# A bidirectional RWKV recurrence laid out anew: direction by half of the partitions, one Gram product for b and k

## The reference, cut to what matters

```
def step(s, inp):
    r_t, w_t, k_t, v_t, a_t, b_t = inp
    sa = jnp.einsum('bhvk,bhk->bhv', s, a_t)
    s = s * w_t[:, :, None, :] + sa[..., :, None] * b_t[:, :, None, :] + v_t[..., :, None] * k_t[:, :, None, :]
    return s, jnp.einsum('bhvk,bhk->bhv', s, r_t)
```

## Time and profile before

| | us |
|---|---|
| median of three runs | 2892.38 |
| the profiled execution | 2887.43 |
| its span, first to last instruction | 2885.4 |
| parameters and first modulation | 0 to 51 |
| projection, to its barrier | about 51 to 460.0 |
| recurrence, to its barrier | 460.1 to 1050.7 |
| the rest (heads, experts, second block) | 1050.7 to 2885.4 |

### The profile page before, as it was taken

The page is one execution under the profiler, slowest core; times in us unless marked ns, Lnnn a source line. Parts: engine busy times, 40 slices in busy tenths (PEclk is TensorE's granted clock), DMA queues, the critical chain, the costliest instruction groups (busy, mean ns, idle before and its releaser), DMA issues. The chain is left out here.

```text
span 2885.4 us, 56115 instructions
## 1 busy us (share of the span) xinstructions
PE 2368.4 (82%) x23980; PEld 1971.1 (68%) x23980; DVE 1720.8 (60%) x2490; ACT 1204.6 (42%) x2180; POOL 612.4 (21%) x528
## 2 busy tenths in 40 slices
PE   5799995889999979692699999998229999777889
PEld 5677785788888857581477777777217777655767
DVE  1555565666666527427588788888346757354652
ACT  2421212444444322242477777777233232255430
POOL 0300002444344300114010111110333544100000
PEclk9799997999999989796799999999659999899999
DMA  5222221110101044336389999998573343000032
GB/s 196 69 71 64 67 65 61 47 47 33 47 33 47 18 151 156 119 124 247 132 329 348 347 352 336 338 349 310 158 262 99 89 146 102 31 1 1 1 124 110
DMA packets 147234, 406.06 MB, mean 141 GB/s; under 512 B 9878, under 2 KB 38700, under 8 KB 146988
## 3 DMA queue, kind: packets, MB, share of 16 engines
q1 hardware_dynamic: 131500, 350.04, 34.0%
q0 software_dynamic: 10880, 39.85, 5.2%
q10 hardware_dynamic: 4608, 12.58, 1.1%
HBM read 350.01 MB, written 52.43 MB: 139 GB/s over the span
## 5 line engine op out<-in xcount | busy, mean ns | idle before, releaser
L1632 DVE TENSOR_TENSOR exp_w_lo<-exp_w,exp_w_hi 128x4096 fp32r<-128x4096 f32 x93 | 410.3, 4424 | 120.1 <-ACT exp_w_hi L1589 118.0
L1589 ACT ACTIVATE exp_w_hi<-exp_w 128x1024 fp32r<-128x1024 f32 x384 | 373.4, 1048 | 175.6 <-DMA exp_w<-in_exp_w_down_dram 91.0
L1958 PE MATMUL bank<-w_hi,h_lo 128*128 128x512 f32 (+1 forms) x448 | 175.4, 391 | 34.3 <-DMA h_lo<-h_tiles 26.1
L1927 POOL TENSOR_TENSOR w_lo<-heads_a,w_hi 128x512 fp32r<-128x512 f32 (+1 forms) x104 | 138.4, 1357 | 184.8 <-ACT w_hi L1973 184.7
L1555 PE MATMUL bank<-exp_w_hi,xsT_lo 128*128 128x512 f32 x512 | 162.2, 398 | 13.5 <-DVE exp_w_lo L1632 7.6
L1958 PE MATMUL bank<-w_hi,h_hi 128*128 128x512 f32 (+1 forms) x448 | 171.6, 383 | 0.0
L1958 PE MATMUL bank<-w_lo,h_hi 128*128 128x512 f32 (+1 forms) x448 | 171.6, 383 | 0.0
L1555 PE MATMUL bank<-exp_w_lo,xsT_hi 128*128 128x512 f32 x512 | 159.3, 393 | 0.0
L1555 PE MATMUL bank<-exp_w_hi,xsT_hi 128*128 128x512 f32 x512 | 158.8, 391 | 0.0
L787 DVE TENSOR_TENSOR w<-bank,const 128x256 f32<-128x256 f32 x200 | 75.4, 419 | 119.5 <-PE bank L1008 119.5
L1523 POOL DMA_INDIRECT moe_rows<-exp_out,idxT x16 | 25.3, 1579 | 562.2 <-DVE exp_out L1683 562.2
(11 more groups left out here) (341 smaller groups left out, 6210.3 us busy)
## 6 DMA issues: line engine op xcount, KB each, us to landing
exp_w<-in_exp_w_gate_dram SPq DMA_DIRECT2D x32, 2048.0 KB, 8.3
exp_w<-in_exp_w_up_dram SPq DMA_DIRECT2D x32, 2048.0 KB, 27.7
exp_w<-in_exp_w_down_dram SPq DMA_DIRECT2D x32, 2048.0 KB, 13.2
heads_a<-in_w_in_dram SPq DMA_DIRECT2D x96, 256.0 KB, 2.8
chunk<-rkv_scratch SPq DMA_DIRECT2D x40, 512.0 KB, 4.1
ada_w_second<-in_ada_w_dram SPq DMA_DIRECT2D x8, 2048.0 KB
w_in_ring<-in_w_in_dram SPq DMA_DIRECT2D x26, 512.0 KB, 4.0
ada_w_first<-in_ada_w_dram SPq DMA_DIRECT2D x4, 2048.0 KB, 11.2
```

Of the source, the lines that this page charges most:

```text
L1589: last = act.activation(wh[:, n % RH, k, :], w[:, n % RING, k, :], ACT.Copy)
L1632: dve.tensor_tensor(wl[:, n % RH, :, :], w[:, n % RING, :, :], wh[:, n % RH, :, :], ALU.subtract).then_inc(lo_ok, 1)
L1927: pool.tensor_tensor(wl[:, q % SR, 0:width(q)], w[:, q % WR, 0:width(q)], wh[:, q % SR, 0:width(q)], ALU.subtract).then_inc(w_lo, 1)
L1958: mm = pe.matmul(g.ps[m % 4][:, 0:cols], lhs[:, t % HT, k, :], rhs[:, q % SR, 0:cols], start=(k == 0 and p == 0), stop=(k == KT - 1 and p ...
```

## The change

1. **Layout.** The forward direction lies on partitions 0 to 63 and the backward direction on 64 to 127; the 8 heads stand side by side. Elementwise work that differed by direction is now one instruction over both (one scan of 512 instead of two of 256), but what writes only one half of the partitions is done twice, once for each half.
2. **Gram.** `bk` holds b, k, b; one product with 128 stationary columns (b and k) gives the rows of both at once. 32 products of 64*64 with 192 moving columns become 16 of 64*128.
3. **128 rows.** `gram[d]` has b's part on one half of the partitions and k's on the other, `uv[d]` has u over v, `sv[d]` state over v. So `r0` and `carry` need one product of 128 rows where they had two of 64, `outputs` one of 64 and one of 128 rows where it had three of 64. The ScalarE copies `a` and `end` into `gram[d]` for that.
4. **v turned in the projection.** TensorE transposes v there (40 transposes), ScalarE copies it out of PSUM in 12 pieces, GpSimd stores it to `v_turned` with 8 DMAs. The recurrence loads it; the 16 products that turned v in each turn are gone, and the mask over their result with them.
5. **Logits** are 32 products of 64*64 on four corners instead of 16 of 64*128.
6. **Parameters** by direction: 12 small DMAs are added in `phase_params` and `w0` is taken out of the old list.

```
@@ phase_params, sync @@
+            for n, name in enumerate(("w0", "a0", "k_a")):
+                for d in range(2):
+                    for half in range(2):
...
+                        sp.dma_start(prow2[row:row + HP, d * C:(d + 1) * C], ...).then_inc(loaded, 16)
@@ phase_project @@
+    FIRST = order.index(("rw", 8))
+    pieces = {n: range(2 * (n - FIRST - 2), 2 * (n - FIRST - 1)) for n in range(FIRST + 2, NT - 1)}
+    pieces[NT - 1] = range(2 * (NT - FIRST - 3), 3 * HP)
+    BLOCKS_OF = (range(0, 4), range(4, 8), range(8, 10))
@@ gpsimd, after the loop over the kept blocks @@
+            for j in range(HP):
+                store_values(j)          # waits for vcopied 3 * j + 3, two DMAs
+            for r in range(2):
+                pool.wait_ge(vstored[r], 32 * HP // 2)
@@ scalar, at block n @@
+                for q in pieces.get(n, ()):
+                    vj, blocks = q // 3, BLOCKS_OF[q % 3]
+                    act.wait_ge(vturned, q + 1)
+                    if vj >= 2:
+                        act.wait_ge(vstored[vj % 2], 32 * (vj // 2))
+                    act.activation(turned_values(vj)[...], g.ps[6 + q % 2][:, 0:len(blocks) * P], ACT.Copy).then_inc(vcopied, 1)
@@ vector, before the mix of a kept block @@
+                        if 10 <= j:
+                            dve.wait_ge(vturned, 3 * (j - 10) + 3)
@@ tensor, after the products of block n @@
+                for q in pieces.get(n, ()):
+                    j, blocks = q // 3, BLOCKS_OF[q % 3]
+                    pe.wait_ge(mixed, FIRST + 1 + j)
...
+                    for k, b in enumerate(blocks):
+                        mm = pe.transpose(g.ps[6 + q % 2][:, k * P:(k + 1) * P],
+                                          mix[:, kept_no[8 + j] % MR, b * P:(b + 1) * P], g.c("ident"))
@@ phase_wkv, scalar: copies into gram[d] @@
+                for d in range(2):
+                    ins = act.activation(v.gram[d][:, 2 * p:2 * p + 2, 2],
+                                         banks[d][:, 0:6 * C].rearrange("p (h a t) -> p h a t", h=2, a=3)[:, :, 2], ACT.Copy)
...
+                    for d in range(2):
+                        ins = act.activation(v.gram[d][HALVES[d], :, 0], v.are[h // 2 % 2][HALVES[d], :, 0], ACT.Copy)
@@ phase_wkv, tensor @@
-                signal(quads(small(s, "P"), [(b.are[i][:, :, 0], state[d][s % 2]) for d, b in enumerate(bs)],
-                             [(b.gk[:, :, 0], b.vT) for b in bs]), s, pe_done)
+                for n in range(NH):
+                    for d in range(2):
+                        mm = pe.matmul(v.B[0][HALVES[d], n * C:(n + 1) * C], v.gram[d][:, n, 0], v.sv[d][:, n], start=True, stop=True)
+            def solve(s):
+                        mm = pe.matmul(v.B[1][HALVES[d], n * C:(n + 1) * C], v.y[HALVES[d], n], v.r0[HALVES[d], n], start=True, stop=True)
+            def carry(s):
+                        mm = pe.matmul(v.B[2][HALVES[d], n * C:(n + 1) * C], v.gram[d][:, n, 2], v.uv[d][:, n], start=True, stop=True)
+            def outputs(s):
+                for j in range(HP):
+                    for half in range(2):
+                        n = HP * half + j
+                        for d in range(2):
+                            pe.matmul(v.B[d][HALVES[half], j * C:(j + 1) * C], v.sv[d][HALVES[d], n], v.are[s // 2 % 2][HALVES[d], n, 1],
+                                      start=True, stop=False)
+                        for d in range(2):
+                            mm = pe.matmul(v.B[d][HALVES[half], j * C:(j + 1) * C], v.uv[d][:, n], v.gram[d][:, n, 1], start=False, stop=True)
+            def products(s):
+                        mm = pe.matmul(v.B[3][HALVES[d], n * C:(n + 1) * C], v.are[s // 2 % 2][HALVES[d], n, 0], v.bk[HALVES[d], n, 0],
+                                       start=True, stop=True)
+            def gram(s, p):
+                        mm = pe.matmul(banks[d][:, 3 * j * C:3 * (j + 1) * C], v.bk[HALVES[d], n, d:d + 2].rearrange("p a t -> p (a t)"),
+                                       v.are[s // 2 % 2][HALVES[d], n].rearrange("p a t -> p (a t)"), start=True, stop=True)
+            def logits(s):
+                            for k in range(2):
+                                mm = pe.matmul(v.Q[k][HALVES[d], n * C:(n + 1) * C], up[HALVES[k], d, c0:c0 + C], g.lora[HALVES[k], c:c + C],
+                                               start=True, stop=True)
```

More of the change, by code:

```diff
@@ L570, in ny, with heads @@
         return (s - NCC) // 2 + 1 if s >= NCC else 0
[L572 to L579 removed]
+    def heads(ap):
+        return ap.rearrange("p (h t) -> p h t", t=C)
     def inside(s):
@@ L718, in taken, with turned @@
[L718 to L721 removed]
+            def turned(s, l):
+                v = group[s % 2]
+                act.wait_ge(pe_done[s % 2], at("pe", s, f"t{l}"))
+                act.activation(v.t[:, :, :, :].rearrange("p j d t -> p (j d t)"), v.Q[0][:, :], ACT.Copy).then_inc(act_done[s % 2], 1)
@@ L871, in _ @@
                 if inside(h + 1):
-                    masked(h + 1, "turnv", "turn")
-                if inside(h + 3):
-                    logits(h + 3, 0)
-                    logits(h + 3, 1)
+                    gram(h + 1, 0)
+                    gram(h + 1, 1)
                 if inside(h):
                     level(h, 4)
+                if inside(s):
+                    dve.wait_ge(exp_done[s % 2], th(s))
+                    n = mark(dve.scalar_tensor_tensor(v.sw, v.a, 1.0, v.pi, ALU.add, ALU.mult))
+                    for d in range(2):
+                        ins = dve.tensor_copy(end[HALVES[d], :], v.gx[HALVES[d], :, 0 if d else C - 1])
+                    ins.then_inc(ends_ok[s % 2], 1)
@@ L888, in _ @@
         def _(pe):
-            def quads(outs, *terms, hps=range(HP)):
-                ends = [None, None]
-                for h in hps:
-                    for i, term in enumerate(terms):
-                        for flip in range(2):
-                            for j in range(2):
-                                half = HALVES[(j + flip) % 2]
-                                st, mv = term[j]
-                                moving = mv[half] if len(mv.shape) == 2 else mv[half, h]
-                                ends[j] = pe.matmul(outs[j][half, h - hps[0]], st[half, h], moving, start=(i == 0), stop=(i == len(terms) - 1))
-                return ends
@@ L1024, in join @@
-                signal(ends, s, pe_done)
+                pe.wait_ge(act_done[s % 2], at("act", s, f"t{l}"))
+                pe.wait_ge(dve_done[s % 2], at("dve", s, f"w{l}"))
+                for j in range(HP):
+                    for d in range(2):
+                        for par in range(2):
+                            mm = pe.matmul(v.Q[par][HALVES[d], j * C:(j + 1) * C], v.t[HALVES[par], j, d], v.w[HALVES[par], d, j],
+                                           start=True, stop=True)
```

704 lines of the change are left out of this document (351 added, 353 removed).

## The result

The changed kernel takes 2904.6 us (median of 9 runs, 2900.3 to 2911.0), the kernel before 2890.2 us (9 runs, 2885.0 to 2901.3): ratio 1.0045, interval 1.0027 to 1.0062. It is slower by 14 us, 0.5%, at the edge of what the prediction called no change; its sum had +2. The profiled execution took 2901.9 us against 2887.4.

The account below looks back on a forecast made before the run. TensorE was taken as the bound, by a small margin. Recurrence -8, projection +6 and start +4 summed to +2 us: 2889 us in the profiled execution's terms, 2894 us as median; range of 8 in 10, 2854 to 2924 us.

Parts of the forecast that it names:

- Start: Before the projection: 11 more loads, 0.34 us apart, all landing before anything starts: +3.7 us (bounds 2 and 6).
- Projection: Whole stage: transposes ahead of the last product block +2.2 us, later v stores +3.7: +6 (bounds +2 and +12).
- GpSimd must store v: End of projection: v stores follow ScalarE's last copies and land 12.6 us after the last product, against 8.9: +3.7.
- The case given for the upper end: End of projection: ScalarE's third v waits for a slot whose store has not landed; the stage's +12 us bound.
- Prologue: Turns before turn 0, at half clock: logits 1.9 us instead of 3.5, v's turning gone: -4 us in the chain.
- Turns 5 to 16: Recurrence turns with outputs: 22.1 us of TensorE work plus waits give 28.1 us against 27.8; +4 us over twelve turns.
- Turns 1 to 4: Recurrence turns without outputs: level-3 products wait for y2; 24.1 us against 25.9; with turn 0, -8 us.
- The last three turns: End of the recurrence: no change, 0 us.
- Rival 1: Outputs: changes of shape inside are free, 2.8 us instead of 5.0, -35 us in all: 2859 us; chance 0.2.
- Rival 2: Solve and a-by-b product: halves sharing a PSUM bank go in turn, 1.86 us not 0.93: 2916 us; 0.3 with Rival 3.
- Rival 3: Recurrence: ScalarE and VectorE take 1 us a turn longer than walked: 2912 us; chance 0.3 together with Rival 2.
- Rival 4: TensorE: the change doesn't save the products it says; no size and no chance of its own given.

Follow-up runs that it names:

- experiment 4: Changed kernel with ScalarE's and VectorE's lists reordered: 2848.5 us; with outputs also regrouped, products of 64 rows before those of 128: 2811.6 us.
- experiment 5: Changed kernel with small parameter loads issued from two queues and the first two turned v's stored early: 2895.8 us; with reordered lists and regrouped outputs too: 2803.6 us.
- experiment 7: Changed kernel without the turning of v (no transposes, copies or waits for them; stores stay, recurrence reads other values): 2901.5 us, ratio 1.0035.
- experiments 1 and 2: Changed kernel with ScalarE's copy y4 ahead of e2: 2888.7 us; changed kernel with four or two unneeded products ahead of z5: 2924.9 or 2896.5 us.
- experiment 3: Changed kernel with outputs' four 64-row products together, then four of 128 rows, 8 changes of shape instead of 16: 2881.1 us, ratio 0.9981.

## Why the prediction was nearly right, and by what

Its time was 2894 us, its range 2854 to 2924; 2904.6 us lies inside. That the 12% less of TensorE's work in a turn (22.1 us for 25.0 in the forecast) comes back as waits on the lists of ScalarE and VectorE is right, and experiment 4 shows it from the other side: with other lists the same products give 56 us, 13 of them by the clock in turns 5 to 16. The size of the difference is less good: +2 us were summed and 14.7 measured. Of the 13 us between the two, 5.4 are the projection, 4.2 the prologue, 0.9 the turns and 2.5 what lies behind them, which the sum doesn't have and whose cause is open. By its steps:

- **Start, +3.7 us:** measured 3.7.
- **Projection, +6 (bounds 2 and 12):** measured 11.4. The step that failed is "GpSimd must store v", which placed the stores behind the copies alone: GpSimd's list has even the first v's store behind its last mix, at 453.59, so the slot that the third v needs comes free late. The case given for the upper end came true: ScalarE's third v waits 2.8 us for it (experiment 5 gives 3.0 us back). The last raw copy to the barrier is 7.3 us longer, for 3.7 forecast. Of the rest, 1.9 us are transposes between products (forecast 2.2), and 1.9 us come from the last eight blocks, which take 14.0 us each instead of 13.76 without any transpose; experiment 7 keeps this, and its cause is open.
- **Prologue, -4:** measured +0.2. The logits did gain 3.4 us, but they were not all of the chain: TensorE waits 4.4 us longer for the features, and later 3.6 us for the first end copies. That the features come later because they are now one piece for both directions is likely, and no run tests it.
- **Turns 5 to 16, 28.1 us:** measured 27.7, which hides two errors of opposite sign. At full clock they are 26.6. The scan was priced at 2.6 us, as two of 256 and with GpSimd beside them, and takes 1.23, which leaves 0.5 to 0.8 of the 2.2 us of wait ahead of join 2. TensorE's own work is 0.7 us more than the 22.1 priced, 0.4 of it because Gram takes 0.85 us a piece with its change against 0.76. The clock puts 1.1 us a turn on top. I had taken the wait of 2.3 us ahead of z5 at its own length only, and it costs 1.5 us more in the seven turns of twelve where the clock falls behind it. "By the clock" was no rival, although showed a low clock where TensorE waits.
- **Turns 1 to 4, 24.1 us:** measured 26.3. Four half-clock stretches, 20.4 us together, lie in them. The rows inside the stretches lose 1.5 us in turn 1 and 1.3 in turn 3, which leaves 24.8 us at full clock, by estimate: of the 2.2 us that are missing, 1.5 are clock and 0.7 TensorE's own work, as in the later turns. That the clock costs this much is weaker here than there: in experiments 1 and 2 the stretches stayed, and so did the wait of 2.56 us ahead of join 3. The reordered kernels have 1.68 us as their longest wait here, fewer stretches, and turns 0 to 4 that are 1 to 4 us shorter; clock and order were not told apart.
- **The last three turns, 0:** measured -4.5, from the opening of turn 17 to the end of the recurrence. They were put at nothing without a reason, and they are more than the whole gain of the turns. The sum of all turns, -3.1 for -4 forecast, is near by luck: turns 5 to 16 came 5 us below it, turns 0 to 4 10 us above, and these 4.5 us below.
- **Small readings:** turning v takes 16 products and 0.93 us (32 records, 753.69 to 754.62), not 32 and 1.87; the product of a and b, also 0.93, is missing beside it, so the 25.0 stands. And 0.51 us for 32 records are 0.016 us a record, not 0.0145, by which the first of the two changes of shape worked out costs 0.10 us; the second gives 0.14 without it, and so does outputs, (5.07 - 8 x 0.348) / 16.
- **Rival 1** (changes of shape inside outputs are free) is refuted by 5.07 us, and experiment 3. The forecast's price for outputs was right to 0.1 us, the products that follow each other on the same columns included; what it did not see is that the order of the products is free, and that another order saves 1.1 us of changes and 1.3 us of products that stand in turn.
- **Rival 2** (what I took to run side by side doesn't) is refuted: 32 records of solve and of r0 take 0.93 us and a change. The halves of solve use different rows of the array and one bank, on different partitions, and still take the 0.029 us a record that they took with a bank each. The Trainium skill (TensorEngine Tiling (Array Packing), Restrictions and Gotchas) says that different row tiles cannot access the same PSUM bank at once; these rows don't bear that out.
- **Rival 3** (1 us a turn longer on ScalarE and VectorE) did not come, though its 2912 us is not far from what was measured: 1.1 us a turn did come, from the clock.
- **Rival 4** (the products are not saved) falls with the page: 21588 records of TensorE instead of 23980.

## What to carry to other kernels

Work taken from the bound engine may shorten a turn only once the lists of its helpers are reordered for the new schedule; here the new products gave all turns together 3 us, and with other lists and outputs regrouped the kernel was 93 us faster than with the lists that came with them. Here an idle stretch of 2.1 us inside a busy stream cost more than its length in seven turns of twelve, since the clock fell behind it: try to split such a wait when it can't be removed, and measure. Before a term is taken from rows, look at what ran beside them. And a term that is put at nothing, as the last three turns were, needs a reason too.

## What the runs showed of the hardware

- One wait of 2.1 us a turn went with stretches of 3.4 us at the 1.2 GHz level in seven turns of twelve, each costing 1.5 us; waits of 0.43 and 1.24 us in its place, or two idle products of 0.9 us each in it, went with none in these turns.
- A change between 64*64 and 128*64 costs 0.14 us (16 of them in outputs' 5.07 us), as for the shapes seen before.
- Products of 128*64 on the two column halves run at once if they stand next to each other: 8 records in 0.39 us with the change, where 4 on the same columns take 0.37.
- Two products of 64*64 on different rows, into one PSUM bank but different partitions, run at once: 32 records of solve in 0.93 us, as with two banks.
- VectorE's scan of 512 that started ahead of GpSimd's instruction took 1.23 us, two of 256 took 2.08; the one that starts second seems to wait until the other is done (an inference from when they end).
